# Moving a token pass's output norm into the pass behind it, through memory

## The reference

```
h2 = rmsnorm(x, g_ffn)
x  = x + jnp.square(jax.nn.relu(h2 @ w_ff1)) @ w_ff2      # 1024 -> 4096 -> 1024
y  = rmsnorm(x, g_final)                                  # the output norm
rmsnorm(x, g) = x * lax.rsqrt(jnp.mean(x * x, axis=-1, keepdims=True) + EPS) * g
```

## Time and profile before

| | |
|---|---|
| Median of 3 runs | 2821.97 us (2818.82 to 2822.32) |
| The profiled execution | 2824.57 us, its span 2822.8 us |
| Busy over the span | TensorE 95%, VectorE 68%, GpSimd 56%, ScalarE 40% |
| Mean granted TensorE clock | 0.981 |
| Chain of work that ended last | TensorE 79%, VectorE 11% |
| Pass 0, pass 1, pass 2 begin | 1425.7, 1872.6, 2341.3 us |
| Pass 2's last product ends | about 2804 us |

### The profile page before, as it was taken

One profiled execution on the slowest core, in us unless ns is written; L12 is line 12 of the kernel. 1 busy time (PEld: TensorE's weight loads), 2 busy tenths in 40 slices (PEclk: granted clock), 3 DMA queues, 4 the chain that ended last, 5 costly groups with the idle time before them and its releaser, 6 DMA issues.

```text
span 2822.8 us, 44241 instructions
## 1 busy us (share of the span) xinstructions
PE 2681.3 (95%) x16558; PEld 2513.9 (89%) x16558; DVE 1912.2 (68%) x3307; ACT 1125.9 (40%) x1944; POOL 1575.9 (56%) x1205
## 2 busy tenths in 40 slices
PE   6999999997999999999989999988999997999997
PEld 4778887786899999999989999977999997999997
DVE  8856567473522657657477778788787688887786
ACT  4212321422232223151264455464554556544554
POOL 3534543554644443354457667655667765677774
PEclk9989999998999999999999999998999999999999
DMA  4555556865455455886234444445545453644443
GB/s 147 165 135 131 133 157 230 246 172 178 148 120 131 120 130 173 213 270 159 69 102 138 136 138 136 138 149 182 136 134 139 136 175 91 202 139 139 139 139 115
DMA packets 271589, 425.45 MB, mean 151 GB/s; under 512 B 26096, under 2 KB 161168, under 8 KB 271248
## 3 DMA queue, kind: packets, MB, share of 16 engines
q1 hardware_dynamic: 190448, 271.29, 32.7%
q0 software_dynamic: 34816, 67.12, 11.1%
q10 hardware_dynamic: 46112, 84.21, 9.1%
HBM read 372.06 MB, written 117.58 MB: 173 GB/s over the span
## 4 chain that ended last, share of the span: by engine, by line
PE 79%; DVE 11%; DVEq 3%; issue 3%; DMA 2%; ACT 2%; ACTq 0%; SPq 0%
PE ps L888 24%; PE ps L890 24%; PE ps L889 23%; DVE r_h L2201 3%; DVE f_h L2201 2%; PE ps L1067 1%; DVEq L2909 1%; DVE f_z L2201 1%; DVE f_g L2201 1%; DVE f_o L2201 1%; PE ps L1152 1%; PE ps L1185 1%; DMA s_constants<-f_m 1%; PE ps L1098 1%; PE ps L1179 0%
## 5 line engine op out<-in xcount | busy, mean ns | idle before, releaser
L889 PE MATMUL ps<-r_h,w_hi 128*128 128x348 f32 (+3 forms) x2632 | 895.1, 340 | 0.0
L821 POOL TENSOR_TENSOR w_hi<-w_raw,zero 128x512 fp32r<-128x512 f32 x200 | 256.1, 1281 | 720.8 <-PE ps L890 688.2
L878 POOL TENSOR_TENSOR w_lo<-f_g,w_hi 128x512 fp32r<-128x512 f32 x336 | 464.7, 1384 | 235.1 <-ACT w_hi L1900 234.4
L878 POOL TENSOR_TENSOR w_lo<-w_raw,w_hi 128x512 fp32r<-128x512 f32 x336 | 457.3, 1362 | 238.2 <-ACT w_hi L1900 237.8
L888 PE MATMUL ps<-r_h,w_hi 128*128 128x512 f32 (+3 forms) x1520 | 535.7, 352 | 31.7 <-DVE r_h L2201 21.3
L890 PE MATMUL ps<-r_h,w_lo 128*128 128x512 f32 (+3 forms) x1520 | 529.4, 348 | 0.0
L889 PEld LDWEIGHTS ps<-r_h,w_hi 128*128 128x128 f32 x2632 | 499.2, 190 | 28.8 <-issue 1.2
L888 PE MATMUL ps<-r_o,w_hi 128*128 128x348 f32 (+1 forms) x1344 | 434.6, 323 | 16.6 <-issue 8.9
L890 PE MATMUL ps<-r_o,w_lo 128*128 128x348 f32 (+1 forms) x1344 | 431.4, 321 | 0.0
L888 PE MATMUL ps<-r_z,w_hi 128*128 128x352 f32 (+3 forms) x1120 | 379.1, 338 | 14.7 <-DVE f_h L2201 12.8
L2201 DVE TENSOR_TENSOR f_z<-f_z,ps 128x348 f32<-128x348 f32 (+3 forms) x704 | 337.5, 513 | 55.8 <-PE ps L890 54.3
(11 more groups left out here) (365 smaller groups left out, 4459.6 us busy)
## 6 DMA issues: line engine op xcount, KB each, us to landing
w_raw<-wpack SPq DMA_DIRECT2D x344, 256.0 KB, 2.8
f_g<-wpack SPq DMA_DIRECT2D x144, 256.0 KB, 2.7
w_raw<-up_sums SPq DMA_DIRECT2D x102, 256.0 KB, 2.6
f_g<-down_sums SPq DMA_DIRECT2D x102, 256.0 KB, 2.7
up_sums<-wpack POOLq DMA_DIRECT2D x48, 512.0 KB, 7.2
down_sums<-wpack POOLq DMA_DIRECT2D x48, 512.0 KB, 8.1
f_g<-up_sums SPq DMA_DIRECT2D x90, 256.0 KB, 2.7
w_raw<-down_sums SPq DMA_DIRECT2D x90, 256.0 KB, 2.7
```

Source lines behind the costliest of these rows:

```text
L821: pool.tensor_tensor(w_hi[:, s, :], rw, zero[:, :].to_broadcast([P, WB]), ALU.subtract).then_inc(w_high, 1)
L878: pool.tensor_tensor(w_lo[:, s, :], raw(s), w_hi[:, s, :].bitcast(F32), ALU.subtract).then_inc(w_split[s], 1)
L889: pe.matmul(out, wh, l, start=False, stop=False, skip_group_check=more)
```

## The change

The norm of pass p (p = 0 and 1) is spread over pass p + 1. The eight tiles go to memory unscaled (`x2_scratch`, `tile_out`), at the first steps of pass p + 1, and x of the new pass takes their place as before. Only tiles 0, 4 and 1 are squared from their place at the end of pass p, into `F_TOTAL`, into slot 0 and into slot 1. The others come back one at a time, in **15 visits** (`VISITS`): visits 0 to 6 add a square, visits 7 to 14 scale a tile. Visits use two slots by turns: an even visit has one piece of 696 columns (`F_SQ`), an odd one two pieces of 348 in what is free elsewhere. ScalarE's queue now issues the loads (`visit_load`, three steps ahead of an adding visit, two ahead of a scaling one) and the stores of the result (`visit_store`, one step behind). In an adding visit ScalarE squares the tile in place one step before. VectorE adds or scales at the visit's step, and waits for the landing in a scaling visit. The sum over channels moves to behind step 0 of (down, 3, 1), the root to its step 1.

```diff
-Y_ROOT = A_G
+Y_ROOT = F_TOTAL
+END_ROOT = A_G
+Y_SLOTS = [[(F_SQ, 2 * SB)], [(A_E + 2 * SB, SB), (F_TOTAL + 2 * SB, SB)]]
...
-SUMS_AFTER = [("up", 0), ("up", 1)]
-SUMS_STEP = [3, 3]
+SUMS_AFTER = [("up", 0), ("down", 3, 1)]
+SUMS_STEP = [3, 0]
...
-SCALE_FROM = 5
+VISITS = [(("down", 0, 1), 5), (("down", 0, 1), 6), (("up", 3), 2), (("down", 1, 1), 6), (("up", 5), 2),
+          (("down", 2, 1), 6), (("up", 7), 2), (("down", 3, 1), 6), (("up", 9), 2), (("down", 4, 1), 6), (("up", 11), 2),
+          (("down", 5, 1), 6), (("up", 13), 2), (("down", 6, 1), 6), (("up", 15), 2)]
+Y_ADDS = KT_D - 1
...
-            def output_store(p, i):
+            def tile_out(p, i):
                 m = Y_TILES[i]
-                sp.wait_ge(y_ready, p * KT_D + i + 1)
-                sp.dma_start(yT[1 - p, :, m * N:m * N + 2 * HALF_TOKENS[p]], x_both(p, m)).then_inc(tile_stored[m], 16)
+                if i < 4:
+                    sp.wait_ge(pairs_read, dve_reads(p, ("down", FF_GROUPS - 1, 1)))
+                else:
+                    sp.wait_ge(pairs_read, dve_reads(p + 1, ITEMS[0]))
+                sp.dma_start(x2_dram[p, m, :, 0:2 * HALF_TOKENS[p]], x_both(p, m)).then_inc(tile_stored[m], 16)
...
             def residual_back(p, i):
                 m, n = Y_TILES[i], 2 * HALF_TOKENS[p + 1]
                 sp.wait_ge(tile_stored[m], 16 * (p + 2))
+                if i < 3:
+                    sp.wait_ge(sq_ready, N_Y[p] * KT_D + i + 1)
...
-                        i = f - (item_at(p, ("up", 1)) + SCALE_FROM + 10)
-                        if 0 <= i < KT_D:
-                            output_store(p - 1, i)
-                        if 0 <= i - 3 < KT_D:
+                        i = f - item_at(p, ITEMS[0]) - 2
+                        if 0 <= i < 4:
+                            tile_out(p - 1, i)
+                        elif 7 <= i < 11:
+                            tile_out(p - 1, i - 3)
+                        if 3 <= i < 7:
                             residual_back(p - 1, i - 3)
+                        elif 10 <= i < 14:
+                            residual_back(p - 1, i - 6)
...
+            def visit_load(p, v):
+                m = Y_TILES[v + 1 if v < Y_ADDS else v - Y_ADDS]
+                y_done(p, v - 2)
+                if v > Y_ADDS:
+                    act.wait_ge(y_ready, KT_D * p + v - Y_ADDS)
+                for place, at, n in visit_parts(v):
+                    act.dma_start(fv(place, n), x2_dram[p, m, :, at:at + n]).then_inc(y_landed, 16)
+
+            def visit_store(p, v):
+                i = v - Y_ADDS
+                act.wait_ge(y_ready, KT_D * p + i + 1)
+                for place, at, n in visit_parts(v):
+                    first = Y_TILES[i] * N + at
+                    act.dma_start(yT[1 - p, :, first:first + n], fv(place, n)).then_inc(results_stored, 16)
+
+            def y_step(p, at):
+                for v, visit in enumerate(VISIT_AT):
+                    if v >= Y_ADDS and at == visit + 1:
+                        visit_store(p, v)
+                for v, visit in enumerate(VISIT_AT):
+                    if v >= 2 and at == visit - (3 if v < Y_ADDS else 2):
+                        visit_load(p, v)
+                    if 2 <= v < Y_ADDS and at == visit - 1:
+                        act.wait_ge(y_landed, y_back(p, v))
+                        y_square(p, v + 1)
...
                             if p and item == SUMS_AFTER[1] and j == SUMS_STEP[1] + 1:
                                 norm_root(N_Y[p - 1], Y_ROOT)
+                            if p:
+                                y_step(p - 1, ITEMS.index(item) * STEPS7 + j)
                             if item[0:2] == ending and p + 1 < PASSES:
                                 i = 7 * item[2] + j
                                 prepare(p + 1, i)
-                                if i in (10, 11, 13):
-                                    y_square(p, (10, 11, 13).index(i))
+                                if i in (9, 11, 13):
...
+                                    y_square(p, (i - 9) // 2)
                             elif p and item == ITEMS[0]:
                                 prepare(p, 14 + j)
-                                if j >= 5:
-                                    y_square(p - 1, j - 2)
-                            elif p and item == ITEMS[1] and j < 3:
-                                y_square(p - 1, 5 + j)
...
-            def y_scale(p, i):
-                m, n = Y_TILES[i], 2 * HALF_TOKENS[p]
-                if i == 0:
+            def y_scale(p, v):
+                m = Y_TILES[v - Y_ADDS]
+                if v == Y_ADDS:
                     norm_root(N_Y[p], Y_ROOT)
-                dve.scalar_tensor_tensor(x_both(p, m), x_both(p, m), vec[:, V_FIN + m:V_FIN + m + 1], fv(Y_ROOT, n),
-                                         ALU.mult, ALU.mult).then_inc(y_ready, 1)
+                dve.wait_ge(y_landed, y_back(p, v))
+                for place, at, n in visit_parts(v):
+                    last = dve.scalar_tensor_tensor(fv(place, n), fv(place, n), vec[:, V_FIN + m:V_FIN + m + 1],
+                                                    fv(Y_ROOT + at, n), ALU.mult, ALU.mult)
+                last.then_inc(y_ready, 1)
...
-                                if i >= 12:
-                                    y_add(p, i - 11)
-                            elif p and item == ITEMS[0] and j >= 5:
-                                y_add(p - 1, j - 2)
-                            elif p and item == ITEMS[1]:
-                                if j < 3:
-                                    y_add(p - 1, 5 + j)
-                                elif j >= SCALE_FROM:
-                                    y_scale(p - 1, j - SCALE_FROM)
-                            elif p and item == ITEMS[2]:
-                                if j + STEPS7 - SCALE_FROM < KT_D:
-                                    y_scale(p - 1, j + STEPS7 - SCALE_FROM)
+                            elif p and (item, j) in VISITS:
+                                v = VISITS.index((item, j))
+                                if v < Y_ADDS:
+                                    y_add(p - 1, v + 1)
+                                else:
+                                    y_scale(p - 1, v)
```

More of the change, by code:

```diff
@@ L342 @@
 Y_TILES = [0, 4, 1, 5, 2, 6, 3, 7]
-SCALE_FROM = 5
+VISITS = [(("down", 0, 1), 5), (("down", 0, 1), 6), (("up", 3), 2), (("down", 1, 1), 6), (("up", 5), 2),
+          (("down", 2, 1), 6), (("up", 7), 2), (("down", 3, 1), 6), (("up", 9), 2), (("down", 4, 1), 6), (("up", 11), 2),
+          (("down", 5, 1), 6), (("up", 13), 2), (("down", 6, 1), 6), (("up", 15), 2)]
+VISIT_AT = [ITEMS.index(_item) * STEPS7 + _step for _item, _step in VISITS]
+Y_ADDS = KT_D - 1
+Y_STORES = 16 * (KT_D // 2 + 2 * KT_D // 2)
 END_SQ = [QKV[FH], QKV[FH] + 4 * SB]
@@ L382, in build @@
     x1_dram = nc.dram_tensor("x1_scratch", (KT_D, P, LEFT_COLS), F32, kind="Internal").ap()
+    x2_dram = nc.dram_tensor("x2_scratch", (PASSES - 1, KT_D, P, 2 * SB), F32, kind="Internal").ap()
     root_dram = nc.dram_tensor("root_scratch", (P, LEFT_COLS), F32, kind="Internal").ap()
@@ L597, in x_both, with y_back, visit_parts @@
             return fv(F_X + m * W, 2 * HALF_TOKENS[p])
+        def y_back(p, v):
+            return 16 * sum(1 + x % 2 for _ in range(p) for x in range(2, len(VISITS))) + 16 * sum(
+                1 + x % 2 for x in range(2, v + 1))
+        def visit_parts(v):
+            parts, at = [], 0
+            for place, n in Y_SLOTS[v % 2]:
+                parts.append((place, at, n))
+                at += n
+            return parts
         def root_of(p, t):
@@ new lines, in y_square, with y_done @@
+                if i == 0:
+                    act.activation(fv(F_TOTAL, 2 * SB), x_both(p, Y_TILES[i]), ACT.Square).then_inc(sq_ready, 1)
+                    return
+                for place, at, n in visit_parts(i - 1):
+                    x = fv(F_X + Y_TILES[i] * W + at, n) if i < 3 else fv(place, n)
+                    last = act.activation(fv(place, n), x, ACT.Square)
+                last.then_inc(sq_ready, 1)
+            def y_done(p, v):
+                if v < Y_ADDS:
+                    act.wait_ge(*((sq_used, 6 * (p + HALVES) + v + 1) if v < Y_ADDS - 1 else (ssum_ready, N_Y[p] + 1)))
+                else:
+                    act.wait_ge(results_stored, 64 + Y_STORES * p + 16 * sum(1 + x % 2 for x in range(Y_ADDS, v + 1)))
@@ L2109, in feed_forward @@
                 for b, t in enumerate((1, 0)):
-                    norm, root = N_Y[PASSES - 1], fv(Y_ROOT + t * n, n)
+                    norm, root = N_Y[PASSES - 1], fv(END_ROOT + t * n, n)
                     act.wait_ge(ms_done, SUM_BASE[norm] + b + 1)
@@ L3021, in end_scale @@
                     x = x_tile(p, m, t)
-                    last = dve.scalar_tensor_tensor(x, x, vec[:, V_FIN + m:V_FIN + m + 1], fv(Y_ROOT + t * n, n),
```

(1 more changed line is left out.)

28 lines of the change are left out of this document (19 added, 9 removed).

## The result

| | before | after | ratio, 95% interval |
|---|---|---|---|
| Median, 6 runs each | 2821.84 us (2817.36 to 2822.32) | 2799.24 us (2792.56 to 2801.67) | 0.9921 [0.9908, 0.9934] |
| Same two kernels on another chip | 2823.06 us | 2796.58 us (2794.89 to 2798.61) | 0.9905 [0.9891, 0.992] |
| The profiled execution, its span | 2824.57, 2822.8 us | 2799.96, 2797.2 us | |
| Mean granted clock | 0.981 | 0.984 | |

Faster, by 22.6 us of median and 24.6 us in the profiled pair. The forecast was 37.6. The time lies inside the forecast range and outside the likeliest case's own (2776 to 2792).

The account below looks back on a forecast made before the run. VectorE's output-norm additions and scalings, with sum and root, were taken to stall TensorE at two pass boundaries. Per boundary 22.7 - 1.9 - 2.0 = 18.8, twice 37.6: 2824.57 to 2787.0, 2784 by the runs; range 2770 to 2803.

Parts of the forecast that it names:

- the likeliest case: Whole kernel: the forecast itself, 37.6 us off, 2784 us by the runs, own range 2776 to 2792; chance 0.60.
- The boundary: First four items of passes 1 and 2: 63.0 us against 85.7, 22.7 us off each, bounds 17.1 and 26.4.
- Item 0: First item after a pass boundary: goes to 20.9 us from 24.8, bounds 1.8 and 6 us off.
- items 1 and 2: Second and third items of a pass: 14.2 and 14.0 us, as waits and most half clock lose their cause.
- near 1.00 in the first 50 us: Start of a pass: sign expected in the profile after, a mean clock near 1.00 over its first 50 us.
- The transfers' place: Steps 2 to 15 of a pass, SP's queue: earlier extra transfers stay hidden; 8 us a pass only if margin shrinks.
- Weights late: Rival, SP's queue: earlier transfers delay weight loads, 16 us more, 2800 us; chance 0.05.
- Sum and root: Behind the first block of (down, 3, 1): moved token sums and root cost 1.9 us a pass, bounds 1.3 and 4.
- the late loads: Four scalings a pass, third step of (up) items: landing at 8.5 us, wait 0.5 each, 2 us a pass (0 to 6).
- The port-bound start: Rival, first four items: VectorE and GpSimd exclude each other, less is gained; 2795.5 us, 2802 if clock falls; chance 0.18.
- The slower rival: Scaling visits: loads land late and hold VectorE before its sums; 2854 us at a 10 us landing; chance 0.04.
- No effect: Rival, items 1 and 2: waits for hidden tiles are their own and stay; 2820 us, chance 0.03.

Follow-up runs that it names:

- b4: Kernel before, with the 15 additions and scalings of each boundary (passes 0 and 1) replaced by a one-column memset that reads no memory; 2801.34 us, 0.9919.
- b6: Kernel before, with the ones-matmuls and root of passes 0 and 1 left out, additions and scalings kept; 2811.97 us, 0.9965.
- b5: Kernel before, with the edits of b4 and b6 together; 2791.44 us, 0.9886.
- e4: Changed kernel, with raw tiles stored and x reloaded at the blocks where the kernel before had them, 16 steps later; 2801.54 us, 0.9924.
- e1: Changed kernel, with each scaling visit's load issued one step earlier, and ahead of the two stores; 2785.17 us, 0.9864.
- b kernels: Six versions of the kernel before, each with part of the old boundary's norm work cut or left out; medians from 2791.44 to 2817.58 us.
- after_again: The changed kernel run once more, unedited, for its spread and a second trace; 2796.58 us, 0.9905.
- b3: Kernel before, with VectorE's additions of squares and scalings of passes 0 and 1 cut to one column each, every wait kept; 2804.8 us, 0.9932.

## Why the prediction was right, and where it was too good

**The boundary was right, in size and by item.** Four items at 63.0 were forecast and 64.5 and 64.1 came: 42.1 us off over two boundaries against 45.4. Item 0 was forecast at 20.9 and took 21.7 to 22.1 in pass 1 of the six profiled executions that have the change; item 1 at 14.2 took 13.4, the steady pace; item 2 at 14.0 took 15.0, which is pass 0's pace; item 3 at 13.9 took 14.2. That items 1 and 2 fit together (28.2 against 28.4) is in part luck, since the one was forecast too long and the other too short. The upper bound of items 1 and 2 was pass 0's 31.4; they took 28.4. One wait was left out of the prediction's account of the clock: it named 6.4 and 4.6 us as the long ones, but the earlier trace rows has one of 5.5, which lies in item 0, and the clock falls there too (0.66 from 1878 to 1886 us). Cut into half microseconds, the trace of before shows 1.00 and 0.50 away from the edges of the low stretches. Around the waits of 5.5, 6.4 and 4.6 us in pass 1 it stands at 0.50 for 6.8, 10.2 and 6.8 us (from 1880.5, 1907.8 and 1938.5), around the same waits in pass 2 for 6.8, 6.8 and 3.4. So it falls near the long waits, but no run shows what length of wait brings how much of it, and the 3 us of loss that two rivals charge for it is the author's estimate. In the changed kernel item 0's longest wait is 1.9 us and its clock is 0.92, not 0.86, with 3.4 us at 0.50. The sign "near 1.00 in the first 50 us" failed there.

**The parts of the cause.** The prediction gave the boundary's loss to VectorE's 19.3 us of additions and scalings and, beside them, the sum and root, without a price for each. Over both boundaries, taking the first out gives 22.3 us (b4: 170.8 to 148.5), the root and its sum alone 13.1 (b6), and both 33.3 (b5), so the two nearly add up. The remaining 8.8 of the 42.1 is 7.7 in item 3, where the transfers have a new place, and 1.1 in the other three. So of VectorE's 38.6 us of work, taking it out was worth 22.3. The 13.1 is not the price of the root's and the sum's own work alone: the wait at the sum goes with them, and a longer one for hidden tiles comes (b6).

**The transfers' place** was costed at nothing in either place, with a price only if TensorE ran at full pace. It did run at full pace, and then the old place would have cost 3.4 us a boundary (e4). The change escaped that because it moved them 17 to 20 steps ahead. The prediction named the new place and gave it no gain, so this part came by luck. Weights late (the rival at 2800) did not come: the blocks of down_sums land in 3.1 us (median from 1874 to 1940 us) against the 4.8 of the earlier trace rows, and from 1874 to 1910 us no engine of the changed kernel is shown waiting for a landing.

**Sum and root**: 1.9 a pass was charged, 1.35 for the matmuls of ones and the rest for banks and weights. Item (down, 3, 1) became longer by 1.17 and 1.18 us, and its neighbours (down, 3, 0) of pass 1 and (down, 4, 0) of pass 2 moved by -0.67 and +0.77. In b5 and b6, without these banks, (down, 4, 0) also goes to 13.9 from 13.2, and in b4, with them, it does not, so this one is the rotation; the -0.67 stays unexplained. The charge was too high by 1.4 us over both passes.

**The step that failed is the size of the late loads.** The mechanism, its four places and its queue were right; its term was 2 us a pass (0.5 a visit, bounds 0 to 1.5) and it measured 4.1 and 4.2 in the profiled execution, 4.4 and 5.6 in the other. By visit in pass 1: 1.3, 0.1, 0.9 and 1.8. The load took 4.6 to 5.5 us to land, not 4.3, in seven of the eight places of the profiled execution. It was issued late in (up, 9) alone, at 5.0 and 5.3 us of the item: there the scaling before it ended late (the first store left at 3.7 and 3.8 us, in most others at 2.8), and the second store held the queue for 0.9 and 1.0 us. In the others it left at 3.7 to 4.1 us, a little earlier than the 4.2 charged. So it landed near 9.9 us of the item in (up, 9), and at 8.5 to 9.2 in the others (once at 7.9), where 8.5 had been forecast for all. The working holds where its numbers do: in (up, 11) of pass 1 the load landed at the forecast 8.5 us, the scaling took 0.94 us, and the item lost 0.1. In (up, 13) the load landed at 8.7, but the scaling took 2.01 us and the item lost 0.9. And (up, 15) was said to add its delay to a loss of 3 us that was there already, but was priced like the rest: it added 1.8 in three of four cases. The visit in (up, 9) of pass 2 passed the bound of 1.5, with 1.7 and 2.0 us in the two executions, and so did (up, 15); the whole stayed within the stated bound of 6 a pass. Removing it (e1) brings 2785.2. That this is next to the forecast 2784 is chance, since the forecast included 4.0 us of it and other terms were off the other way.

**The rest of the gap.** Between 37.6 and the 24.6 of the profiled pair lie 13.0 us: 3.3 from the boundary, 4.3 from the late loads, 1.0 from (down, 7, 1), -1.4 from sum and root, 1.0 outside the span (2.8 us around it against 1.8), and 4.1 from the clock at the ends of passes: (down, 7, 0) took 16.2, 16.1 and 16.0 us in the three passes against 14.7, 15.0 and 14.5 before. That leaves 0.7, mostly pieces of about 0.1 us in the (down, g, 0) items. Two larger pieces happen to cancel: (up, 0) of pass 0, where nothing was changed, took 2.3 us more (21.4 against 19.2, at a clock of 0.84 against 1.00), and the part before it 2.2 us less. The clock's part is at least not fixed by the change: in the second execution of the same kernel the same item took 14.7, 15.0 and 14.8, and in pass 0, where nothing was changed, two of the b kernels (b4, b5) show 16.2 too. Stretches of these items, first the profiled execution, then the second:

```profile
1844.70:1860.80 16.10, 16.10 (x84) 16.10 (x85) 12.46 (x22) 11.30 (x21) 8.68 (x7) 0.81 0.57 178
```
```profile
1844.10:1858.90 14.80, 14.75 (x85) 14.78 (x86) 13.24 (x22) 11.31 (x21) 8.72 (x7) 0.90 0.67 210
```

In passes 1 and 2 items of 15.8 us or more came only in kernels with late loads (after, e4_late_transfers), though not in after_again, which has them too; whether those raise its chance stays open.

**Rivals.** The port-bound start is not what happened as a whole: item 1 ran at the steady pace, below pass 0's, and item 0 took 21.9, between the forecast and the rival's 23. It was right on items 2 and 3, which took pass 0's 15.0 and 14.2. Of the exclusion that it builds on, the traces show this. Beside a split, a VectorE operation with two inputs in SBUF took longer (a one-column addition up to 1.08 us against 0.16, b3). One with a single such input did not (`f_h<-f_h,ps` in the kernel before: 0.50 us at 1892.88 within a split, 0.51 at 1911.67 with none), nor did the memsets of b4 (0.06). The other way round, the split that began at 1884.64 in b4, while VectorE's r_m of 1884.50 ran, took 1.90 us, the one at 1893.95, with none of VectorE's beside it, 1.29. The slower rival had the right place and the wrong landing: it needed 7 us from issue, and 3.8 to 5.5 were measured. Its 7 does not follow from its own terms either, which bring the 3 us of half clock only behind a wait of 4.6 us, a landing some 8.4 us after issue. "No effect" is out.

## What to carry to other kernels

When work leaves a crowded stretch, the bound there is a chain through several queues, so cut it one part at a time and then together: here the parts gave 22 and 13 us of 42 (33 together), and most of the rest, 7 us, showed only as a transfer that the lateness had been hiding. A reload placed by step must be read as time of issue, with everything ahead of it in the issuing queue, plus landing, plus what stands behind the waiting engine; here one step earlier and ahead of the stores was worth 10 us by the items and 11 by the median. Prefer sums over items to medians when what you look for is one microsecond.

## What the runs showed of the hardware

- What a GpSimd split added to a VectorE operation with two inputs in SBUF did not shrink with the operation: 0.92 us in both additions. An addition of 696 columns took 0.88 us free and 1.80 beside a split (1873.78 in the kernel before), one of a single column 0.16 free and up to 1.08 (1898.40 in b3_neither), a scaling of one column 0.22 and up to 1.26 (1911.07 there). A one-column memset took 0.06 us always (b4_no_slots).
- The same 3.0 us pause of TensorE before (down, 7, 0) was followed in pass 0 of one execution by a mean clock of 0.81 over the item and in another by 0.90, for the same kernel: 1.4 us an item that no edit explains. In the kernel before, with a pause as long, it was 1.00.
- Issuing two stores in a row on ScalarE's queue took 0.34 us for the first and 0.46 for the second in most places, but up to 1.03 (after) and 1.49 us (e1_load_early) for the second in (up, 9): one such pair does not give the price of another.
